# Where the sums of a norm's scale and shift run: both moved into the norm's gap, in place of filler matmuls

## What is computed

```
c_act = jax.nn.silu(c)
for l in range(DEPTH):                                    # DEPTH = 2
    mod = (c_act @ w_mod[l] + b_mod[l])[:, None, :]       # w_mod[l] is 1024 x 6144
    sh1, sc1, gt1, sh2, sc2, gt2 = jnp.split(mod, 6, axis=-1)
    h = rmsnorm(x, norm1_g[l]) * (1 + sc1) + sh1
    ...                                                   # three token mixers, merged by gates
    x = x + gt1 * (merged @ w_out[l])
    h2 = rmsnorm(x, norm2_g[l]) * (1 + sc2) + sh2
    x = x + gt2 * conv_gated_mlp(h2, ffn_up[l], ffn_conv_w[l], ffn_conv_b[l], ffn_down[l])
return rmsnorm(x, final_g)
```

## Time and profile before

| | |
|---|---|
| median of 3 runs | 1142.48 us |
| the profiled execution: its own time, its span | 1142.95 us, 1141.2 us |
| mean granted PE clock over the span | 0.995 |
| PE busy | 1117.2 us (98%) |
| DVE busy, ACT busy | 827.5 us (73%), 574.1 us (50%) |

### The profile page before, as it was taken

How to read it: one execution, slowest core, us unless ns; L and a number is a source line. 1 busy time by engine, 2 the same in 40 slices (tenths; PEclk the granted TensorE clock), 3 DMA queues, 4 the chain that set the end, 5 groups by cost and what they waited for, 6 DMA issues and landing times.

```text
span 1141.2 us, 24125 instructions
## 1 busy us (share of the span) xinstructions
PE 1117.2 (98%) x10096; PEld 1016.2 (89%) x10096; DVE 827.5 (73%) x1233; ACT 574.1 (50%) x885; POOL 124.3 (11%) x140
## 2 busy tenths in 40 slices
PE   8999999999999999999999999999999999999997
PEld 7889987888789999999988899887886999999996
DVE  5798988654476888987626798967636867778763
ACT  2357467522274666663422565782226556666533
POOL 0000000155002000001100000002530100000001
PEclk9999999999999999999999999999999999999999
DMA  9965445353145466668845456351613455555651
GB/s 376 367 222 188 168 168 219 112 173 127 75 148 222 177 235 217 233 209 321 304 134 184 161 184 220 145 203 61 217 46 148 167 203 185 184 184 184 219 188 38
DMA packets 40952, 214.35 MB, mean 188 GB/s; under 512 B 7680, under 2 KB 8064, under 8 KB 21536
## 3 DMA queue, kind: packets, MB, share of 16 engines
q1 hardware_dynamic: 29344, 171.13, 41.1%
q0 software_dynamic: 11520, 41.95, 10.7%
HBM read 212.01 MB, written 1.05 MB: 187 GB/s over the span
## 4 chain that ended last, share of the span: by engine, by line
PE 92%; DVE 4%; ACT 2%; issue 1%; DMA 1%; SPq 0%; DVEq 0%; ACTq 0%
PE ps L1671 16%; PE ps L1672 16%; PE ps L1673 16%; PE ps L1691 9%; PE ps L1861 6%; PE ps L1863 6%; PE ps L1867 5%; PE ps L1965 5%; PE ps L1640 2%; DMA R<-wmod_dram 1%; PE ps L2142 1%; PE ps L1956 1%; PE ps L1656 1%; PE ps L1943 1%; PE ps L1888 1%
## 5 line engine op out<-in xcount | busy, mean ns | idle before, releaser
L907 ACT ACTIVATE WH<-ring 128x1024 fp32r<-128x1024 f32 x144 | 151.6, 1058 | 176.6 <-PE ps L1673 164.8
L1540 DVE TENSOR_TENSOR WLO<-ring,WH 128x1024 fp32r<-128x1024 f32 x144 | 175.7, 1230 | 79.6 <-ACT WH L907 79.6
L1671 PE MATMUL ps<-HH,WH 128*128 128x256 f32 x736 | 208.3, 283 | 0.0
L1672 PE MATMUL ps<-HL,WH 128*128 128x256 f32 x736 | 208.3, 283 | 0.0
L1673 PE MATMUL ps<-HH,WLO 128*128 128x256 f32 x736 | 208.3, 283 | 0.0
L1671 PEld LDWEIGHTS ps<-HH,WH 128*128 128x128 f32 x736 | 141.3, 192 | 0.0
L1672 PEld LDWEIGHTS ps<-HL,WH 128*128 128x128 f32 x736 | 141.3, 192 | 0.0
L1673 PEld LDWEIGHTS ps<-HH,WLO 128*128 128x128 f32 x736 | 141.3, 192 | 0.0
L532 POOL DMA_DIRECT2D mring<-wmod_dram x80 | 43.7, 547 | 780.1 <-DVE macc L1050 415.5
L1671 PE MATMUL ps<-GH,WH 128*128 128x256 f32 x384 | 108.9, 284 | 0.0
L1672 PE MATMUL ps<-GL,WH 128*128 128x256 f32 x384 | 108.7, 283 | 0.0
(11 more groups left out here) (396 smaller groups left out, 2475.6 us busy)
## 6 DMA issues: line engine op xcount, KB each, us to landing
ring<-wmain_dram SPq DMA_DIRECT2D x150, 1024.0 KB, 4.9
mring<-wmod_dram POOLq DMA_DIRECT2D x80, 512.0 KB, 5.0
G<-wmod_dram SPq DMA_DIRECT2D x3, 1024.0 KB, 9.9
R<-wmod_dram SPq DMA_DIRECT2D x3, 1024.0 KB, 17.6
TK<-wmod_dram SPq DMA_DIRECT2D x2, 1024.0 KB, 20.6
X<-x_t_dram SPq DMA_DIRECT2D x1, 1024.0 KB, 5.7
SW<-small_dram SPq DMA_DIRECT2D x2, 512.0 KB, 10.3
y_dram<-H SPq DMA_DIRECT2D x4, 256.0 KB, 2.2
```

What stands on the lines that cost most here:

```text
L907: A(WH[:, n % 2, part], ring[:, b, part], ACT.Copy).then_inc(hi_ready, 1)
L1540: V.tensor_tensor(WLO[:, n % 2, part], ring[:, b, part], WH[:, n % 2, part].bitcast(F32), ALU.subtract).then_inc(lo_ready, 1)
L1671: MM(out, w_high[:, at], high, start=start, stop=False, skip_group_check=True)
L1672: MM(out, w_high[:, at], low, start=False, stop=False, skip_group_check=True)
```

## The change

Both sums of a norm now run in its gap, one behind the other, and `keep_clock` is taken out of the three gaps.

- PE: `mod_sum(6l + 3)` leaves the merge and stands behind `ones_sum`, ahead of `mod_sum(6l + 4)`; `mod_sum(6)` leaves the down-projection and stands behind `ones_sum(2)`, ahead of `mod_sum(7)`. The transposes into banks 6 and 7 wait for one vector less.
- DVE: the scale's vector and `norm_gain` stand directly ahead of `norm`; the shift's vector is read inside `norm`, behind its first tile.

```diff
-DN_SUMS = [{2: 5, 4: 6}, {8: 11}]
+DN_SUMS = [{2: 5}, {8: 11}]
...
-            def norm(n, A_):
+            def norm(n, A_, unit=None):
                 after()
                 dve.wait_ge(x_rt, n + 1)
                 for m in range(KT):
+                    if unit is not None and m == 1:
+                        mod_vector(unit)
                     V.scalar_tensor_tensor(H[:, m, :], X[:, m, :], A_[:, m:m + 1], RT[:, :], ALU.mult, ALU.mult).then_inc(h_pre, 1)
...
                 if l:
-                    mod_vector(7)
-                norm(2 * l, Acol)
+                    mod_vector(6)
+                    norm_gain(col(1, "n1g", 0, 8), 6)
+                norm(2 * l, Acol, 7 if l else None)
...
                 gated(4)
-                mod_vector(6 * l + 3)
...
-                norm_gain(col(l, "n2g", 0, 8), 3 if l == 0 else 9)
                 for j in range(4):
...
-                mod_vector(6 * l + 4)
-                norm(2 * l + 1, Acol)
+                mod_vector(6 * l + 3)
+                norm_gain(col(l, "n2g", 0, 8), 3 if l == 0 else 9)
+                norm(2 * l + 1, Acol, 6 * l + 4)
...
-                if l == 0:
-                    norm_gain(col(1, "n1g", 0, 8), 6)
...
                 pe.wait_ge(gn_rt, 2 * (l + 1))
-                mod_sum(6 * l + 3)
...
                     if half:
-                        pe.wait_ge(mod_ready, 6 * l + 4)
+                        pe.wait_ge(mod_ready, 6 * l + 3)
...
                 out(3, 0, KT)
+                mod_sum(6 * l + 3)
                 mod_sum(6 * l + 4)
-                keep_clock(4, 6, C[:, 0:S])
...
                 if l == 0:
+                    mod_sum(6)
                     mod_sum(7)
-                    keep_clock(4, 6, C[:, 0:S])
```

## The result

| | before | after |
|---|---|---|
| median of six runs each, us | 1142.64 (1142.43 to 1144.15) | 1149.61 (1146.33 to 1151.5) |
| profiled execution, span, us | 1142.95, 1141.2 | 1146.33, 1144.4 |
| mean granted clock of the span | 0.995 | 0.987 |

The ratio is 1.0041 (95% interval 1.0024 to 1.0058): the change makes the kernel slower by 4.7 us (2.7 to 6.6). The plain difference of the two medians is larger, 7.0 us. The forecast was 1144.0 with a range up to 1146.8: the sign of its middle case was right, the size is outside the range by either figure (1142.6 + 4.7 = 1147.3, and 1149.61).

The account below looks back on a forecast made before the run. PE was taken as the bound, 92% of the chain that ended last. -5.1 + 3.8 + 2.8 = +1.5 us on the profiled 1142.95 gave 1144.4, or 1144.0 on the median's terms; range 1140.5 to 1146.8.

Parts of the forecast that it names:

- middle case: The clock falls in each of the three gaps at the middle price: +1.5 us in all, 1144.0; chance 0.52.
- What leaves: -5.1: Three sums leave PE's row, in both merges and the down-projection, 1.70 us each: 5.1 us off.
- feared wait: PE waiting for merged tiles in the merge (slack 0.1) or low weights in the down-projection (slack 0.9).
- rivals with the freed time lost: Merge's 1.7 not passed on, +4.9 (1147.4), or down-projection waits for low weights, +3.2 (1145.7); chance 0.09 together.
- The later start: +3.8: In each gap the second sum waits for the scale's vector, so the product starts 1.28 later; three gaps, +3.8.
- The clock: +2.8: PE's clock falls to half in each of the three gaps: 0.6 + 0.6 + 1.6 = 2.8 us.
- taken: 0.6: Cost of the clock's fall in each gap before an up-projection, 0.6 us, between bounds 0 and 1.7.
- 1.6 between the layers: Cost of the clock's fall in the gap between the layers, about one stretch, between bounds 0 and 3.0.
- early falls: Rival: clock falls during the second sum in all three gaps, 6.4 instead of 2.8; +5.1, 1147.6; chance 0.17.
- The 3.0 allowed for two stretches in a row: Upper bound of the clock's cost between the layers: two half-clock stretches less the waiting between, 3.0 us.
- the 1.7 was one stretch: Upper bound of the clock's cost before an up-projection: half of a 3.4 us half-clock stretch, 1.7 us.
- "Slower": Outcome of the whole kernel above 1144.8 us, about 0.2% (2.3 us) over before; chance 0.36.

Follow-up runs that it names:

- six traces: Profiles of six executions of the changed kernel, no edit between them; the three gaps cost 7.4 to 11.6 us together, 9.2 in the mean.
- 5.7 in the second: The changed kernel timed again without edit, beside before on the same chip: 1149.78 against 1144.04 us, ratio 1.0050.
- Q kernels: Four kernels, wide sums except in gaps under study: before's order 1143.24; after's order 1148.69, with middle gap wide 1145.66, with outer gaps wide 1146.85 us.
- sixth trace: Another profile of the changed kernel, no edit; its three gaps cost 4.40, 4.26 and 1.67 us.
- fifth trace: Another profile of the changed kernel, no edit; its three gaps cost 1.56, 5.78 and 4.26 us.
- kernel with quiet surroundings: Before with wide sums everywhere except in the three gaps, which keep one one-column sum and the filler: 1143.24 against before's 1144.07 us, ratio 0.9990.

## Why the prediction was wrong

**What leaves: -5.1, right.** The three sums are worth 1.7 to 1.8 each in every trace of after, 5.1 to 5.3 together. Neither feared wait came: the transposes follow at once, with the 0.1 of slack that was counted, and PE's waits list nothing on `merged` or, in the down-projection, on low weights. The rivals with the freed time lost are out.

**The later start: +3.8, nearly right.** The second sum starts 2.19 behind the first (forecast 2.15), the product 1.37 later (forecast 1.28); three times that is 4.1. Acol was ready before the root, as forecast.

**The clock: +2.8, the step that failed.** That it falls in each gap was right in 18 gaps of 18. The Trainium skill ("TensorE: Matmul & The Clock Gate", on why this matters for kernels) would keep the clock by leaving no long idle gap of PE between bursts of matmuls. The traces of after do not agree: no idle piece of PE in these gaps is longer than 0.95, and the clock falls nonetheless. Taking 1.37 off each gap of the six traces leaves, in the mean, 0.75 for each of the two before an up-projection (taken: 0.6) and 3.6 for the one between the layers (taken: 1.6). Together 5.1, and -5.1 + 4.1 + 5.1 = +4.1, against 4.7 (2.7 to 6.6) in the first timing and 5.7 in the second. The Q kernels bear out, apart from any trace, that the clock costs microseconds in the middle gap (3.0) and in the other two together (1.8). That the middle gap carries most of it is shown by the traces of after alone, where it does in five of six.

So the term that was mis-sized is the 1.6 between the layers, "about one stretch", which measured 3.6. One stretch was never seen there, but two or three. The prediction saw both parts of the mechanism and priced them in different cases: the stretching of the second sum (3.08 to 3.45 in five of the six traces, where 1.92 is normal) went into the rival "early falls", the half-clock product into the middle case. Between the layers they come together in those five, since the fall comes early in the second sum and the clock is not back before 6.8 or 10.2 us are over; in the sixth trace the two stretches lie over the product alone. The upper bounds were too low as well. The 3.0 allowed for two stretches in a row, and with three it is 5.78 - 1.37 = 4.4; before an up-projection the 1.7 was one stretch, and two gaps of twelve, with three, cost 2.9 and 3.0. "About one stretch" rested on the single one of the earlier trace rows, which had 2.0 us of wide matmuls right behind it; here PE went from the sum into 0.95 of waiting and then into a product whose tiles ACT hands over one by one. That this is why the clock stays down longer is my reading; no run changed it alone.

The rival "early falls" was the nearest to the result, with +5.1 and 0.17. In its form it is not what happened: it had all three gaps alike, and in the six traces of after the fall comes early before an up-projection in two cases of twelve only.

**The probabilities.** "Slower" had 0.36. With 1.5 to 4.5 for the middle gap and the other terms as they were, the sum would have been +1.4 to +4.4, and slower, which begins at +2.3, the likeliest.

**What stays open.** At PE's end the six traces of after lie 6.2 behind before's in the mean (1.5 to 9.3), and only 4.1 of that is from the steps above. The other 2.1 are from elsewhere: at the start, where they have one to three stretches at half clock against one; falls at about 209 and 772 us (1.4 each, in two and three of the six); and a wait of PE for ACT at about 750 us (1.0, fifth trace). Part of this is before's single trace, at 1142.95 and a clock of 0.995 against medians of 1143.6 to 1144.1 and a clock of 0.992 to 0.993 in the later timings: before has such falls too in some executions, as its kernel with quiet surroundings did (three stretches at 19 us, and one each in two of its gaps). Whether the change makes falls outside the gaps likelier was not tried. Nor is it settled what makes those at the start: they stay in some traces where all sums there are wide. And the kernel with wide sums in its gaps is 1.9 over before where 0.5 under was expected from its gaps and sums; its trace shows where 2.3 went, not that it always does.

## What to carry to other kernels

Before a step is moved into a gap, ask what PE streams in that gap as well as how long it waits there; a filler that looks free can be what holds the clock for the next product, and removing it alone cost 7 us here. Where small sums must stand there, give them wide operands (128 identical columns cost 0.1 us more a sum than one) and a bank of their own: with that, and all other sums wide too, the moved order went from 1.0050 of before's time to 0.9980. Price a fall of the clock by what PE does behind it: in the kernel without filler a single stretch cost 0.40 before an up-projection, where ACT sets the pace, and 1.73 between the layers, where PE's own matmuls do. Allow for two or three stretches in a row.

## What the runs showed of the hardware

- With PE busy on one-column f32 matmuls the granted clock falls to 0.50 (1.2 GHz): in 18 of 18 gaps of after, in six traces, with idle pieces of 0.35 and 0.95 us. With 128 columns there was no fall in any of 15 gaps, in seven traces, with the same idle pieces or only the 0.95.
- The half-clock stretches in these traces last 3.4, 6.8 or 10.2 us, and the same place of one kernel gets another number of them from run to run: 2, 2, 3, 3, 3, 2 between the layers.
- A sum of eight f32 matmuls with 128 x 128 weights takes 1.95 us with 128 columns and 1.84 with one. The sixteen weight loads of a first sum take 1.97 us in either case; that they pace it is my reading.
- The mean granted clock of the timed runs (0.985 against 0.993) gave 5.1 more half-clock stretches a run for after than for before; its six traces have 5.2 in the three gaps.
